# Grid attention: the products of probabilities and values, cut over the queries into two halves of TensorE's columns

## What is computed

```python
        s = jnp.einsum('bnqhd,binchd->bnhqic', q_r.reshape(B, ncb, NA_COL_BLOCK, H, Dh), k_r) + bias
        s = jnp.where(col_mask[:, None, :, None, :], s, NEG_INF)
        p = jax.nn.softmax(s.reshape(B, ncb, H, NA_COL_BLOCK, kh * NA_KEY_COLS), axis=-1)
        o = jnp.einsum('bnhqic,binchd->bnqhd', p, v_r)
```

## Time and profile before

| what | value |
|---|---|
| median of three runs | 5913.16 us |
| profiled execution, its span | 5914.6 us |
| the same execution's own time apart from the span | not given; runs of the kernel are 5903.86 to 5920.61 us |
| PE busy in the span | 5484.3 us (93%) |
| DVE, ACT, POOL busy | 3843.9, 2866.8, 1282.9 us |
| grid attention, about 4071 to 4601 us of the span | 530 us |
| output products of grid attention (line 2452) | 2304 matmuls, 277 ns mean life |

### The profile page before, as it was taken

How to read it: one execution, slowest core, us unless ns; L and a number is a source line. 1 busy time by engine, 2 the same in 40 slices (tenths; PEclk the granted TensorE clock), 3 DMA queues, 4 the chain that set the end, 5 groups by cost and what they waited for, 6 DMA issues and landing times. The chain is left out here.

```text
span 5914.6 us, 101032 instructions
## 1 busy us (share of the span) xinstructions
PE 5484.3 (93%) x31546; PEld 4720.4 (80%) x31547; DVE 3843.9 (65%) x6597; ACT 2866.8 (48%) x4819; POOL 1282.9 (22%) x957
## 2 busy tenths in 40 slices
PE   7999999999899979699999879998999897999997
PEld 5888788898899978578788637988999685788773
DVE  5677877778555558676766467774444555655785
ACT  3343443445477766265655313444666213645671
POOL 2010020000000000064656330200000003544673
PEclk9999999999999989799999989999999897999998
DMA  6776776668799976377888475654443426876987
GB/s 183 207 199 196 205 218 202 186 179 208 240 322 312 308 242 182 132 286 269 333 295 293 173 285 171 200 158 127 155 122 115 132 82 213 303 254 239 342 305 280
DMA packets 888282, 1309.42 MB, mean 221 GB/s; under 512 B 186014, under 2 KB 547149, under 8 KB 887948
## 3 DMA queue, kind: packets, MB, share of 16 engines
q1 hardware_dynamic: 756060, 939.81, 50.5%
q0 software_dynamic: 77168, 294.67, 14.6%
q10 hardware_dynamic: 54720, 70.60, 3.6%
HBM read 974.87 MB, written 348.87 MB: 224 GB/s over the span
## 5 line engine op out<-in xcount | busy, mean ns | idle before, releaser
L520 PE MATMUL qa_ps_out<-qa_x_hi,qa_w_hi 128*128 128x512 f32 x1344 | 533.5, 397 | 39.7 <-DVE qa_w_lo L644 24.0
L520 PE MATMUL qa_ps_out<-qa_x_hi,qa_w_lo 128*128 128x512 f32 x1344 | 528.4, 393 | 0.0
L520 PE MATMUL qa_ps_out<-qa_x_lo,qa_w_hi 128*128 128x512 f32 x1344 | 528.4, 393 | 0.0
L557 ACT ACTIVATE qa_w_hi<-qa_w_whole 128x1024 fp32r<-128x1024 f32 x180 | 191.3, 1063 | 443.0 <-DVE qa_w_whole L635 259.3
L520 PE MATMUL qa_ps_out<-qa_w_hi,qa_x_hi 128*128 128x256 f32 x1344 | 383.1, 285 | 6.5 <-DVE qa_w_lo L644 6.5
L520 PE MATMUL qa_ps_out<-qa_w_lo,qa_x_hi 128*128 128x256 f32 x1344 | 381.5, 284 | 0.0
L520 PE MATMUL qa_ps_out<-qa_w_hi,qa_x_lo 128*128 128x256 f32 x1344 | 381.5, 284 | 0.0
L1991 POOL TENSOR_TENSOR b_ex_w_lo<-b_ex_w_raw,b_ex_w_hi 128x1024 fp32r<-128x1024 f32 x128 | 351.5, 2780 | 134.1 <-ACT b_ex_w_hi L1988 130.1
L1991 POOL TENSOR_TENSOR a_ex_w_lo<-a_ex_w_raw,a_ex_w_hi 128x1024 fp32r<-128x1024 f32 x128 | 350.8, 2771 | 131.8 <-ACT a_ex_w_hi L1988 125.3
L2485 DVE CUSTOM_DVE_ANT_0 ga_minus_s<-ga_ps_s,ga_bias 128x512 f32<-128x512 f32 (+1 forms) x256 | 193.9, 758 | 266.3 <-PE ga_ps_s L2428 254.2
L1010 PE MATMUL da_ps_o<-da_v_two,da_probT 128*128 128x130 f32 x2560 | 356.1, 278 | 1.6 <-DMA da_v_two<-v 1.6
(11 more groups left out here) (442 smaller groups left out, 15780.4 us busy)
## 6 DMA issues: line engine op xcount, KB each, us to landing
a_ex_w_raw<-w SPq DMA_DIRECT2D x128, 1024.0 KB, 12.6
b_ex_w_raw<-w SPq DMA_DIRECT2D x128, 1024.0 KB, 12.2
qa_w_raw<-w_qkv_a SPq DMA_DIRECT2D x144, 512.0 KB, 4.3
a_ex_w_raw<-w POOLq DMA_DIRECT2D x66, 1024.0 KB, 9.1
b_ex_w_raw<-w POOLq DMA_DIRECT2D x66, 1024.0 KB, 8.7
da_q_cross<-qT SPq DMA_DIRECT2D x48, 1024.0 KB, 9.0
da_k_parts<-kT SPq DMA_DIRECT2D x48, 1024.0 KB, 10.0
ys<-qa_x_rows POOLq DMA_DIRECT2D x64, 512.0 KB, 4.1
```

Of the source, the lines that this page charges most:

```text
L520: done = pe.matmul(out, stationary, moving, start=(k == 0 and i == 0), stop=(k == KH - 1 and i == 2))
L557: act.activation(w_hi[:, p % W_RING], src, ACT.Copy).then_inc(w_hi_done, 1)
```

## The change

Each chunk product of `outputs` becomes two. Each takes 64 of the 128 queries as stationary columns and writes 64 partitions of `ps_o`; the one for the first 64 queries is placed at column 0 of the array, the other at column 64 (`tile_position`). The moving operand is only the 65 columns of the job's own head, and they go to the same columns of `ps_o` as before. Waits, signals and all else stay.

```diff
+                    own = slice((HD + 1) * head, (HD + 1) * head + HD + 1)
                     for c in range(n):
-                        done = pe.matmul(ps_o[:, j % 2, 0:V_COLS], probT[:, j % 2, c, :], v_two[:, u % 2, c0 + c, :],
-                                         start=(c == 0), stop=(c == n - 1))
+                        for side in range(2):
+                            rows_of = bass.ts(side, HD)
+                            done = pe.matmul(ps_o[rows_of, j % 2, own], probT[:, j % 2, c, rows_of],
+                                             v_two[:, u % 2, c0 + c, own], start=(c == 0), stop=(c == n - 1),
+                                             tile_position=(0, HD * side))
                     done.then_inc(summed, 1)
```

## The result

The changed kernel takes 5871.09 us (median of four runs, 5858.40 to 5875.74) against 5915.20 us beside it: ratio 0.9924, 95% interval 0.9911 to 0.9938, so 44 us less, with 37 to 53 by the interval. It is faster, by 0.8%. I had forecast 5990 and slower; the time lies in the stated range (5830 to 6120), on its other side.

A forecast was written before the change was run, and what follows sets the result against it. PE was taken to bound the grid attention stage, busy 529 of 530 us. Serial passes, +19 us, and switches, +60, made +79 us on 5914.6, 5994, stated as 5990 us; range 5830 to 6120.

The forecast's parts named there:

- The bound: Grid attention: PE busy 529 of 530 us, ACT 350; a nanosecond on PE moves the end by a nanosecond.
- The clock of one pass: Grid attention's output products: passes start 0.112 us apart; streaming 130 columns and loading 128 take equally long.
- Load and stream halved, their number doubled: Grid attention's output products: 4608 loads of 64 columns, about 0.057 us each, and 4608 passes of 65 columns.
- If the halves follow one another: Grid attention's output products: passes run serially, 0.06 us apart, mean +0.075 us a job, +19 us taken.
- rival A: Grid attention's output products: both halves run side by side, -111 us; 5803, 5863 or 5924 us by switch price; chance 0.34.
- The switches: Grid attention: PE changes between whole and halved array 512 times, costing nothing to 120 us; middle, +60 us, taken.
- Rival B: Grid attention: products serial, changes between whole and cut array free; 5912 to 5934 us, mostly same; chance 0.14.
- C: Grid attention's output products: narrow pieces cost as much as wide ones (6151 us) or loads are not hidden (6173); chance 0.12.
- D: Grid attention: half-used columns lower the clock, PE's 530 us becoming some 1060, total 6445 us; chance 0.04.
- ACT next: Grid attention with halves overlapping: ACT 1.37 us a job against PE's 1.64, so the gain would stand, barely.

The follow-up runs named there:

- the run with both heads' columns: The changed kernel with each half of the queries streaming 130 columns instead of 65: 5986.1 us, ratio 1.0123.
- The halves in turn: The changed kernel with its two loops swapped, all chunks of the first 64 queries before those of the other 64: 5945.87 us, ratio 1.0060.
- Four quarters: The changed kernel with four cuts of 32 queries in place of two of 64, same 65 columns: 5899.1 us, ratio 0.9965.

## Why the prediction was wrong

**The bound** was right: PE ends the stage, and its 51.0 us less are the result's 44 within its interval.

**The clock of one pass** was right: load and stream equally long. (The 0.117 us of the ten passes was read as a step; the single records have one first step of 0.160 us and then 0.112.) The rows of before show it for the load only; that a stream of 130 columns takes 0.11 us by itself came out of the run with both heads' columns. Streams alone halved save 11 us; pieces of half the width with full streams save nothing.

**Load and stream halved, their number doubled**: right; a pass of 65 columns starts 0.058 us after the one before it on its half.

**"If the halves follow one another"** is the step that failed. It put the passes in one row, +19 us in the sum, and made that the likeliest case (0.36 against 0.34 for rival A). In its place the runs show two passes in a slot of 0.058 us, which is -115 us. The argument was that both halves read the same 128 partitions, and that the rows show one load of 128 columns at a time, 0.11 us. But those rows are of an undivided array; they say nothing of whether two halves have a path each. They have, for loads and streams: twenty passes in ten slots. The halves in turn, which come nearest to the single row that the forecast assumed, stay 80 us above. I had written "if the load path is one", a condition that no row tests, and then let the nearest row decide. The wrong direction is this step alone: with -115 in place of +19 the same sum is faster.

**The switches** were priced at 0 to 0.47 us a job, with the middle, 0.23, taken. Measured: 0.27 with full streams, and 0.25 in the changed kernel's trace: by its rows, 0.20-0.11 going in, 0.15-0.11 coming out, and 0.05 or so at either edge where the first load stands uncovered (the transposes' five take 0.77 us instead of 0.71). So 60 us were taken and 63 to 69 measured. That the middle came so near is luck: it was a halfway point between two bounds, not a mechanism. The upper end had the next load wait for a product's whole life, 0.39 or 0.27 us; it waits for less, 0.33 after a product of 512 columns and 0.20 after one of 128. The Trainium skill, page "TensorEngine Tiling (Array Packing)", section Tiling Modes, says that a change of mode drains TensorE. The trace agrees in that no load is placed ahead across the change, at about half of the price that I gave to a full drain.

**Rival A** was worked out at -111 us and, with the middle price, 5863 us. Measured are 5871 us; in the stage's trace the overlap gives -115 and the switches take 63, together -52 against the 51.0 us measured. Had it been the forecast, the time would have been right to 8 us.

**Rival B** is out: the switch is not free. **C** is out: the loads of narrow pieces are hidden and cost half. The Trainium skill, page "TensorE: Matmul & The Clock Gate", section Part 3, has loads overlap products in flight only where the row group differs. The trace contradicts this a second time, with a cut array: the twenty loads over the same 128 rows take 0.67 us beside the passes. **D** is out: granted 1.00.

**ACT next**: expected barely covered. DVE's new wait for ACT and PE's 1.0 us for ACT's copy say the same.

## What to carry to other kernels

Where weight loads and streams of full-width fp32 products are equally long (here 0.11 us each) and only half of the streamed columns are needed, cutting the stationary operand over two halves of the array and alternating them product by product halves the products' time. Count in about 0.25 us for each round trip between the cut and the whole array. By an estimate from these numbers (0.25 over the 0.054 us that a pass saves) a group of products must be longer than some five undivided passes to gain; no run tested that length cleanly. Before gathering work to save such switches, look at what queues behind it on the other engines: here the gathering cost 60 us until one copy was moved. And when no row shows a resource in the state that the change puts it in, do not let the nearest row choose between "one" and "two": price both cases and say that the direction of the forecast is open between them.

## What the runs showed that I had not expected

The engine reaches ahead between halves: with all products of one half issued first, the second half's started 0.17 us, three steps, before the first half was through. Four quarters run together as two halves do, but in that run PE paused 16 times with nothing that it waited for, and each pause ended about 2.5 us after a packet of instructions had started. An instruction stream twice as long seems to bring them. And in the dilated stage the faster products bring out a wait for the queries' load that was hidden before, 0.8 us there and 6.0 to 17.8 with the products cut.
